# Fetching each expert's rows by one gather, the body for few tokens per expert first, and x turned last

## What is computed

```python
for layer in range(DEPTH):
    sh1, sc1, g1, sh2, sc2, g2 = jnp.split(jax.nn.silu(c) @ p['ada_w'][layer] + p['ada_b'][layer], 6, axis=-1)
    h = modulate(rmsnorm(x, p['norm_mix'][layer]), sh1, sc1)
    ...
    x = x + g1[:, None, :] * out
    h = modulate(rmsnorm(x, p['norm_ffn'][layer]), sh2, sc2)
    ...
    x = x + g2[:, None, :] * f
# the experts (layer 1)
logits = (h @ w_router).astype(jnp.float32) + b_router.astype(jnp.float32)
top_val, top_idx = lax.top_k(logits, TOP_K)
top_w = jax.nn.softmax(top_val, axis=-1)
gates = jnp.sum(jax.nn.one_hot(top_idx, N_EXPERTS, dtype=jnp.float32) * top_w[..., None], axis=-2)
for e in range(N_EXPERTS):
    y = y + gates[..., e:e + 1] * swiglu(h, w_gate_up[e], w_down[e])
```

## Time and profile before

| what | us |
|---|---|
| median of 3 runs | 1758.15 (1756.03 to 1758.58) |
| the profiled execution | 1758.0 |
| its span | 1756.3 |
| PE busy | 1612.5 (92%) |
| DVE busy | 1265.2 (72%) |
| ACT busy | 1077.6 (61%) |
| GpSimd busy | 88.9 (5%) |
| mean DMA rate | 311 GB/s |

### The profile page before, as it was taken

One profiled execution on the slowest core, in us unless ns is written; L12 is line 12 of the kernel. 1 busy time (PEld: TensorE's weight loads), 2 busy tenths in 40 slices (PEclk: granted clock), 3 DMA queues, 4 the chain that ended last, 5 costly groups with the idle time before them and its releaser, 6 DMA issues.

```text
span 1756.3 us, 25170 instructions
## 1 busy us (share of the span) xinstructions
PE 1612.5 (92%) x9156; PEld 1304.0 (74%) x9156; DVE 1265.2 (72%) x1442; ACT 1077.6 (61%) x1302; POOL 88.9 (5%) x135
## 2 busy tenths in 40 slices
PE   6999587999887798699999999999999999999992
PEld 2983277999776557488888888888888888888882
DVE  3653364555547525399899899898998998998983
ACT  3643243443434444477787777877777777777771
POOL 2000110000003300100000000000000000000001
PEclk9999888999998899799999999999999999999995
DMA  9458949554376995899999999999999999999972
GB/s 347 163 192 314 391 140 317 192 177 171 112 286 237 384 333 197 302 345 367 367 380 368 383 373 363 387 372 371 379 373 377 368 370 386 367 366 386 374 266 98
DMA packets 241092, 546.25 MB, mean 311 GB/s; under 512 B 6131, under 2 KB 28785, under 8 KB 241026
## 3 DMA queue, kind: packets, MB, share of 16 engines
q1 hardware_dynamic: 229202, 504.42, 79.2%
q0 software_dynamic: 11184, 38.75, 5.9%
q10 hardware_dynamic: 640, 2.18, 0.4%
HBM read 522.56 MB, written 22.75 MB: 310 GB/s over the span
## 4 chain that ended last, share of the span: by engine, by line
PE 83%; DMA 7%; DVE 5%; ACT 2%; issue 1%; POOL 1%; SPq 0%; POOLq 0%; ACTq 0%; DVEq 0%
PE psum L737 24%; PE psum L738 24%; PE psum L739 24%; PE psum L705 2%; DMA ring<-in_ada_w 2%; DMA ring<-in_cache_k 2%; PE psum L1172 1%; DVE w_lo L1621 1%; DMA ring<-in_ffn_w_gate_up 1%; DVE ring L1923 1%; PE psum L689 1%; PE psum L976 1%; PE psum L723 1%; DMA routed<-h_tok,row_of 1%; PE psum L1166 1%
## 5 line engine op out<-in xcount | busy, mean ns | idle before, releaser
L2095 DVE TENSOR_TENSOR w_lo<-ring,w_hi 128x1024 fp32r<-128x1024 f32 x672 | 813.2, 1224 | 83.4 <-ACT w_hi L1563 67.4
L1563 ACT CAST w_hi<-ring 128x1024 fp32r<-128x1024 f32 x672 | 706.0, 1053 | 207.4 <-PE psum L739 194.2
L737 PE MATMUL psum<-w_hi,xe_hi 128*128 128x512 f32 x896 | 360.3, 402 | 2.9 <-DVE w_lo L2095 2.9
L739 PE MATMUL psum<-w_hi,xe_lo 128*128 128x512 f32 x896 | 356.1, 397 | 0.0
L738 PE MATMUL psum<-w_lo,xe_hi 128*128 128x512 f32 x896 | 356.1, 397 | 0.0
L737 PE MATMUL psum<-hh,w_hi 128*128 128x264 f32 x864 | 251.7, 291 | 35.7 <-DVE w_lo L1621 23.2
L1621 DVE TENSOR_TENSOR w_lo<-ring,w_hi 128x1024 fp32r<-128x1024 f32 (+1 forms) x132 | 160.1, 1222 | 140.0 <-ACT w_hi L1251 139.9
L738 PE MATMUL psum<-hl,w_hi 128*128 128x264 f32 x864 | 248.1, 287 | 0.0
L739 PE MATMUL psum<-hh,w_lo 128*128 128x264 f32 x864 | 248.0, 287 | 0.0
L1251 ACT CAST w_hi<-ring 128x1024 fp32r<-128x1024 f32 (+1 forms) x132 | 135.6, 1034 | 125.5 <-PE psum L739 85.9
L737 PEld LDWEIGHTS psum<-w_hi,xe_hi 128*128 128x128 f32 x896 | 169.5, 189 | 42.4 <-DVE w_lo L2095 3.3
(11 more groups left out here) (362 smaller groups left out, 1416.0 us busy)
## 6 DMA issues: line engine op xcount, KB each, us to landing
ring<-in_moe_w_gate_up SPq DMA_DIRECT2D x112, 2048.0 KB, 9.3
ring<-in_moe_w_down SPq DMA_DIRECT2D x56, 2048.0 KB, 8.6
ring<-in_ada_w SPq DMA_DIRECT2D x24, 2048.0 KB, 11.3
ring<-in_ffn_w_gate_up SPq DMA_DIRECT2D x22, 1024.0 KB, 8.8
ring<-in_gla_w_in SPq DMA_DIRECT2D x6, 2048.0 KB, 10.5
ring<-in_kv_ada_w SPq DMA_DIRECT2D x4, 2048.0 KB, 8.0
ring<-in_ffn_w_down SPq DMA_DIRECT2D x4, 2048.0 KB, 7.9
ring<-in_kv_w SPq DMA_DIRECT2D x4, 2048.0 KB, 12.9
```

The lines of the kernel that those rows point to most:

```text
L737: eng.matmul(to, wh, ah, start=start, stop=False)
L739: return eng.matmul(to, wl, ah, start=False, stop=stop)
L1563: eng.copy(unit(w_hi, kind, n), quarter(ring[(BASE + j // 4) % RING], kind, j % 4)).then_inc(S["hi_ready"], 1)
L2095: eng.tensor_tensor(unit(w_lo, kind, n), quarter(ring[(BASE + j // 4) % RING], kind, j % 4), unit(w_hi, kind, n), ALU.subtract).then_inc(S ...
```

## The change

- The zeros and their eight DMAs go. `h_tok` is written to a plain DRAM buffer `h_rows` by three DMAs on ACT's queue (`send_rows`), without an index.
- Each expert's 128 rows are fetched by one indirect DMA on GpSimd's queue. The token numbers come from PE: for expert `e` DVE writes `picks[e]` (one where a token has place `c` in the expert), three operations of 128 columns, and `find` multiplies them with `token_no`, three matmuls of one column. Expert 0 is found ahead of the branch, experts 1 to 7 behind it, before the first `turn_rows`. Unused places point to row 0 in place of zeros.
- The two bodies change places; the comparison is turned round.
- Turning `x` and copying it to `x_tok` moves behind the loop over the experts. `x_tok` and `y_g` hold picks before.
- Modulation tiles 28 to 31 run whole (`ada_whole`, 8 matmuls) and at other places: 28 and 29 behind the sums of squares, 30 ahead of the counts, 31 behind `find(0)`. `row_back` is made inside the body.

```diff
-ADA_GROUPS = ((0, (0, 1)), (4, (2, 3)), (16, (4, 5)), (18, (4, 5)), (20, (6, 7)), (22, (6, 7)), (28, (2, 3)))
+ADA_GROUPS = ((0, (0, 1)), (4, (2, 3)), (16, (4, 5)), (18, (4, 5)), (20, (6, 7)), (22, (6, 7)), (28, (2, 3)), (30, (0, 1)))
...
-            eng.memset(zero_rows[:], 0.0).then_inc(S["consts"], 1)
-            eng.wait_ge(S["consts"], 12 + STRIPS)
-            for e in range(NE):
-                eng.dma_start(routed[e * T:e * T + CAP, :], zero_rows[0:CAP, :]).then_inc(S["routed_zero"], 16)
-            eng.wait_ge(S["routed_zero"], 16 * NE)
             eng.tensor_copy(ident_r[:], ident[:]).then_inc(S["att_consts"], 1)
...
-            eng.wait_ge(S["h_tok_kept"], 2 * TT)
-            eng.wait_ge(S["rows_placed"], 1)
-            for t in range(TT):
-                for c in range(2):
-                    eng.indirect_dma_start(routed, row_index(row_of, t, c), h_tok[0:TOK[t], t, :], None).then_inc(S["rows_sent"], 16)
+                eng.indirect_dma_start(xe_rows[:], None, h_rows,
+                                       bass.IndirectOffsetOnAxis(row_from[:, e:e + 1], 0)).then_inc(S["expert_rows"], 16)
+
+            eng.wait_ge(S["h_rows_sent"], 16 * TT)
+            eng.wait_ge(S["rows_placed"], 2)
+            expert_rows(0)
             eng.wait_ge(S["most_ready"], 1)
             busiest = eng.value_load(most[0:1, 0:1], min_val=0, max_val=T)
...
-            with eng.If(busiest > cap):
...
-            with eng.Else():
-                eng.wait_ge(S["rows_sent"], 16 * 2 * TT)
-                expert_rows(0)
+            with eng.If(busiest <= cap):
                 eng.wait_ge(S["last_sent"], 16)
                 for n in range(3):
                     eng.dma_start(row_bc[:, n, :], last_rows[n].partition_broadcast(P)).then_inc(S["last_spread"], 16)
+                eng.wait_ge(S["rows_placed"], 4)
                 eng.wait_ge(S["xe_turned"], 2)
                 expert_rows(1)
...
-            ada(112, 116)
...
+            def ada_whole(i):
+                landed(eng, "ada", i)
+                ada_strips(i, 0)
+                ada_strips(i, 1)
+
+            eng.wait_ge(S["ada_kept"], 28)
+            ada_whole(28)
+            ada_whole(29)
...
-            turn_h(0)
-            turn_h(1)
+            ada_turn(28)
+            ada_turn(29)
             eng.wait_ge(S["lg_kept"], 1)
             for t in range(TT):
                 last = eng.transpose(pb[5][0:TOK[t], t * NE:(t + 1) * NE], lg8[:, t * P:t * P + TOK[t]], ident[0:NE, 0:NE])
             last.then_inc(S["lg_turned"], 1)
-            for i in range(2, 2 * TT):
-                turn_h(i)
+            turn_h(0)
+            turn_h(1)
+            ada_whole(30)
             eng.wait_ge(S["gates_ready"], 1)
...
-            ada(116, 128, ends=True)
+            for i in range(2, 2 * TT):
+                turn_h(i)
+
+            def find(e, bank):
+                for t in range(TT):
+                    last = eng.matmul(bank[:, e:e + 1], picks[e][0:TOK[t], t, :], token_no[0:TOK[t], t:t + 1],
+                                      start=t == 0, stop=t == TT - 1)
+                return last
+
+            eng.wait_ge(S["rows_placed"], 1)
+            find(0, pb[4]).then_inc(S["rows_found"], 1)
+            ada_whole(31)
+            ada_turn(30)
+            ada_turn(31)
             eng.wait_ge(S["most_ready"], 1)
             busiest = eng.value_load(most[0:1, 0:1], min_val=0, max_val=T)
-            with eng.If(busiest > cap):
...
                 eng.wait_ge(S["last_gains"], 1)
                 for n, row in enumerate((mod[:, GATE[FFN1]:GATE[FFN1] + KC, 0], gain[:, FINAL, :, 0],
                                          mod[:, SHIFT[FINAL]:SHIFT[FINAL] + KC, 0])):
-                    last = eng.transpose(pb[4][0:KC, n * P:(n + 1) * P], row, ident[:])
+                    last = eng.transpose(pb[2][0:KC, n * P:(n + 1) * P], row, ident[:])
                 last.then_inc(S["once_turned"], 1)
...
+                eng.wait_ge(S["rows_placed"], 3)
+                for e in range(1, NE):
+                    last = find(e, pb[3])
+                last.then_inc(S["rows_found"], 1)
                 eng.wait_ge(S["expert_rows"], 16)
-                eng.wait_ge(S["once_kept"], 5)
-                turn_rows(0)
+                turn_rows()
...
-                            turn_rows(it * 2 + 2)
-
+                            turn_rows()
+
+                for i in range(4):
+                    t, a = i // 2, i % 2
+                    for j in range(4):
+                        last = eng.transpose(pb[i][:, j * P:(j + 1) * P], x[:, 4 * a + j, t * P:(t + 1) * P], ident[:])
+                    last.then_inc(S["once_turned"], 1)
...
+            norm(FFN1, splits=False, after=(S["kept_dve"], empt[-1][1]), during=(112, 120))
+            ada_copy(29)
...
-            for i in range(2 * TT):
...
+            def keep_h_tok(i):
                 t, a = i // 2, i % 2
                 eng.wait_ge(S["h_tok_turned"], i + 1)
                 eng.copy(h_tok[0:TOK[t], t, a * 512:(a + 1) * 512], pb[6 + i % 2][0:TOK[t], :]).then_inc(S["h_tok_kept"], 1)
+
+            def send_rows(t):
+                eng.wait_ge(S["h_tok_kept"], 2 * t + 2)
+                eng.dma_start(h_rows[t * P:t * P + TOK[t], :], h_tok[0:TOK[t], t, :]).then_inc(S["h_rows_sent"], 16)
+
+            keep_h_tok(0)
+            keep_h_tok(1)
             eng.wait_ge(S["gates_exp"], 1)
             eng.activation(e2[:, 0:TT], e2[:, 0:TT], ACT.Exp).then_inc(S["gates_exp_done"], 1)
-            ada(116, 128, ends=True)
+            send_rows(0)
+            ada_copy(30)
+            eng.preload_act_table_set("silu_and_others")
+            for i in range(2, 2 * TT):
+                keep_h_tok(i)
+                if i >= 4:
+                    send_rows(i - 3)
+            ada_copy(31)
             eng.wait_ge(S["most_ready"], 1)
             busiest = eng.value_load(most[0:1, 0:1], min_val=0, max_val=T)
...
-                eng.wait_ge(S["once_turned"], 5)
-                eng.copy(last_kept, pb[4][0:KC, 0:3 * P]).then_inc(S["once_kept"], 1)
-                eng.wait_ge(S["once_kept"], 5)
...
+            with eng.If(busiest <= cap):
...
+                for i in range(4):
+                    eng.wait_ge(S["once_turned"], i + 2)
+                    eng.copy(x_tok[:, i // 2, i % 2 * 512:(i % 2 + 1) * 512], pb[i]).then_inc(S["once_kept"], 1)
...
-            ada(112, 116)
             norm(FFN1)
...
+            ada_add(28)
+            ada_add(29)
...
-                last = eng.scalar_tensor_tensor(slot_f[0:n, t, :], iota[0:n, 0:NE], float(T), pb[5][0:n, t * NE:(t + 1) * NE],
-                                                ALU.mult, ALU.add)
+                last = eng.tensor_copy(slot_f[0:n, t, :], pb[5][0:n, t * NE:(t + 1) * NE])
             link(last)
-            eng.tensor_tensor(slot_of_hit[:, 0, :, :], slot_f[:], hit[:], ALU.mult)
-            link(eng.tensor_tensor(slot_of_hit[:, 1, :, :], slot_f[:], hit2[:], ALU.mult))
-            link(eng.tensor_reduce(slot_sum[:], slot_of_hit[:].rearrange("p c t e -> p (c t) e"), AX.X, ALU.add))
-            eng.tensor_copy(row_of[:], slot_sum[:]).then_inc(S["rows_placed"], 1)
+
+            def pick_rows(e):
+                for t in range(TT):
+                    n = TOK[t]
+                    last = eng.scalar_tensor_tensor(picks[e][0:n, t, :], iota[0:n, 0:CAP], slot_f[0:n, t, e:e + 1],
+                                                    chosen[0:n, t, e:e + 1].to_broadcast([n, CAP]), ALU.is_equal, ALU.mult)
+                return last
+
+            pick_rows(0).then_inc(S["rows_placed"], 1)
             link(eng.tensor_reduce(w1[:, 7:8], pb[5][:, TT * NE:(TT + 1) * NE], AX.X, ALU.max))
             eng.tensor_copy(most[:], w1[:, 7:8]).then_inc(S["most_ready"], 1)
+            eng.wait_ge(S["rows_found"], 1)
+            eng.tensor_copy(row_from[:, 0:1], pb[4][:, 0:1]).then_inc(S["rows_placed"], 1)
+            for e in range(1, NE):
+                last = pick_rows(e)
+            last.then_inc(S["rows_placed"], 1)
...
-            ada(116, 128, ends=True)
+            ada_add(30)
+            ada_add(31)
             busiest = eng.value_load(most[0:1, 0:1], min_val=0, max_val=T)
-            with eng.If(busiest > cap):
...
+            with eng.If(busiest <= cap):
...
+                link(eng.scalar_tensor_tensor(slot_f[:], experts, float(CAP), slot_f[:], ALU.mult, ALU.add))
+                eng.tensor_tensor(slot_of_hit[:, 0, :, :], slot_f[:], hit[:], ALU.mult)
+                link(eng.tensor_tensor(slot_of_hit[:, 1, :, :], slot_f[:], hit2[:], ALU.mult))
+                link(eng.tensor_reduce(slot_sum[:], slot_of_hit[:].rearrange("p c t e -> p (c t) e"), AX.X, ALU.add))
+                eng.tensor_copy(row_back[:], slot_sum[:])
+                eng.wait_ge(S["rows_found"], 2)
+                eng.tensor_copy(row_from[:, 1:NE], pb[3][:, 1:NE]).then_inc(S["rows_placed"], 1)
...
                 for t in range(2):
```

(20 more changed lines are left out.)

265 lines of the change are left out of this document (131 added, 134 removed).

## The result

| | median us (range) | ratio to the kernel before |
|---|---|---|
| kernel before, same chip | 1757.61 (1756.03 to 1758.58) | |
| changed kernel | 1739.32 (1736.7 to 1740.91) | 0.9897 (95% interval 0.9885 to 0.9908) |
| changed kernel, measured again | 1739.95 (1735.73 to 1742.58) | 0.9911 (0.9894 to 0.9929) |

The forecast was 1746.8 with a range of 1740.5 to 1752.5. The profiled execution took 1739.41 us, its span is 1737.7.

A forecast was written before the change was run, and what follows sets the result against it. TensorE, busy without a gap in the experts' loop, was taken as the bound, so only an earlier loop start helps: 1758.0 - 9.9 (dense mixer gap) - 1.3 (way to the first expert) = 1746.8 us, range 1740.5 to 1752.5.

The forecast's parts named there:

- Part 1: Start of the dense channel mixer, PE's gap at 271.5 to 281.4 us: dropping the zeros gives -9.9 us.
- The landing: Second `ffn_up` tile's load, issued at 261.7 us: arrives 8.2 us later, at 269.9 in place of 278.7.
- the clock: PE's granted clock behind the gap near 271 us: no fall to half after a 1.2 us gap, -1.4 us.
- the split: DVE's splitting of weights at 260.03 us, now beside GpSimd's attention constants: +0.3 us, at most 0.9.
- Rival (e): Gap near 271 us: the tile is slow by itself in 1 KB packets, no gain there; 1756.7 us, chance 0.02.
- (b): Second `ffn_up` tile still lands late, at the median 12.0 us: +3.8, perhaps +1.4 for clock; 1750.6 to 1752, chance 0.12.
- Part 2: Norm and router: the root starts 1.8 us later, the counts end near 707.0 us, +1.6.
- the root: ACT's root of the norm: waits for the copy of modulation column 28, 691.1 in place of 689.30 us, +1.8.
- Part 3: Finding and fetching, counts to first expert: PE comes to the rows at 729.6 in place of 730.86 us, -1.3.
- Rival (c): Write and then gather among 2 MB weight tiles: rows come 22 us late, 1770 us; chance 0.04.
- Rival (a): PE's clock stays up while finding tokens: 4.8 us less there, another 2.9 in the first expert; 1739.1, chance 0.15.
- Rival (d): Slow picks before the first expert and a far-page fetch at the kernel's end (+3): +4, 1752.1 us; chance 0.09.

## Why the forecast was wrong, and where it was right

**Part 1** held: -10.3 forecast as -9.9. The landing was put at 8.2 us and took 7.71; the clock did not fall; beside GpSimd's constants the split took 1.31 us where it had taken 1.23, 0.08 us more and not 0.3. Rival (e), and (b) in this place, are out: the zeros moved away and the zeros put back shift the gap in opposite directions.

**Part 2**: the root was delayed by 1.83 us as worked out (+1.8). The counts came 1.6 us earlier than forecast against it, 1.45 of which was the logits' clock in that execution; without this luck the part costs 1.4.

**Part 3** held, in the order of its steps and in its sum: 22.5 us from counts to turning against 22.6. The picks took 5.6 (5.0), the finding 9.87 (9.2), and DVE's register load with what follows it 0.99 (2.0; the load alone 0.55 us where it had taken 1.64): that the sum is right to 0.1 us is in part luck, since these misses cancel. Rival (c) is refuted: in the run that finds as it picks write and gather were through by 710.2, 16.8 us after the counts, and in the changed kernel PE doesn't wait for them. Rival (a) is refuted by the clock of 0.50 over the finding; its time, 1739.1, is nearly the measured one, for another reason. Rival (d) is out: DVE's last work to the end of the span is no longer than before.

**The step that failed** is in the first paragraph: "The change leaves the instructions of this loop alone, so whatever moves the start of the loop moves the end of the kernel by as much." The instructions stayed, their operands moved, and the loop, which the sum holds at nothing, became 3.5 us shorter. That is 3.5 us of the 7.4 by which trace and forecast differ, shown by the run that moved the tiles alone. With them added back the measured time is 1742.8, inside the range. The rest: 1.45 logits, 0.8 ahead of the tile, 0.4 in part 1, and 1.0 behind the last turning. The last isn't the change either: the kernel before has that stretch as short in its second trace. The range had no term for what differs between executions. Of the 12 to 16 us that the change is worth at equal addresses 11.2 were forecast; what is above that the runs don't place.

## What to carry to other kernels

A change that adds or removes an SBUF tile moves all that is laid out behind it, and here the pace of a matmul-bound loop hung on this: compare the period of the loop in both traces before any stage is explained, and try a few paddings ahead of the stationary tiles, since here 96 bytes were worth some 24 us, more than the whole change. A burst of large writes that nobody waits for was paid here by the one load that is waited for; spread out, the same bytes cost nothing that was seen. Where an engine must make many small things that another waits for, let the second take each as it comes, ahead of a branch rather than behind it.

## What the runs showed of the hardware

- The spacing of 512-column fp32r matmuls hung on the SBUF address of the stationary operand: 118.48 to 121.95 us for the same work, 2.9%, at a granted clock of 1.00 and with weight loads of 188 ns in both. Other tiles' addresses gave 0.1 us.
- PE's granted clock fell to 0.50 while PE was busy 2.00 of 2.00 us, with one-column matmuls (1.00, 0.66, 0.50 from 700 to 706 us) and, in the one trace of it, also with 264-column products between them.
- After a branch to the far body DVE stood still for 6.36 us, after one to the near body for 0.99.
